# A narrow gate tile in plain fp32, in four column parts, behind the first tile of a hybrid encoder's first projection

## What is computed

```python
h = rms_norm(x, p['norm_mix'][layer])
proj = h @ p['ev_w_in'][e]
u, q, k, v, og, glr = jnp.split(proj, EV_SPLITS, axis=-1)   # 512, 256, 256, 512, 512, 32 columns
y_s5 = s5_mixer(u, ...)
y_gla = gla_mixer(q, k, v, og, glr, ...)
...
# in gla_mixer
lr = glr.astype(f32).reshape(bsz, L, 2, GLA_RANK)
logit = jnp.einsum('blzr,zrk->blzk', lr, w_gate.astype(f32)) + b_gate.astype(f32)
```

## Time and profile before

| | us |
|---|---|
| median of 3 runs (2389.73 to 2390.05) | 2390.03 |
| profiled execution | 2389.74 |
| its span, first to last instruction | 2388.0 |
| TensorE busy | 2377.4 |
| VectorE busy | 1544.8 |
| ScalarE busy | 1165.8 |
| start of the trunk's first tile on TensorE | 232.06 |

### The profile page before, as it was taken

The page is one execution under the profiler, slowest core; times in us unless marked ns, Lnnn a source line. Parts: engine busy times, 40 slices in busy tenths (PEclk is TensorE's granted clock), DMA queues, the critical chain, the costliest instruction groups (busy, mean ns, idle before and its releaser), DMA issues.

```text
span 2388.0 us, 34322 instructions
## 1 busy us (share of the span) xinstructions
PE 2377.4 (100%) x13607; PEld 2009.3 (84%) x13607; DVE 1544.8 (65%) x2616; ACT 1165.8 (49%) x2060; POOL 0.2 (0%) x4
## 2 busy tenths in 40 slices
PE   9999999999999999999999999999999999999999
PEld 6988877888889888987788888888888898888887
DVE  8999668776477876664666438958885565433332
ACT  5334455555445565545454436646764453533432
POOL 0000000000000000000000000000000000000000
PEclk9999999999999999999999999999999999999999
DMA  5435632553224654443225223232324323323322
GB/s 202 107 97 160 217 110 85 178 207 118 63 87 150 194 188 138 133 133 106 80 92 170 92 88 124 89 106 97 98 98 150 115 88 116 124 98 97 97 97 88
DMA packets 109695, 291.28 MB, mean 122 GB/s; under 512 B 18944, under 2 KB 40576, under 8 KB 108256
## 3 DMA queue, kind: packets, MB, share of 16 engines
q1 hardware_dynamic: 100832, 264.83, 34.4%
q10 hardware_dynamic: 8704, 24.25, 3.1%
HBM read 267.45 MB, written 19.50 MB: 120 GB/s over the span
## 4 chain that ended last, share of the span: by engine, by line
PE 87%; DVE 2%; ACT 1%; issue 0%; ACTq 0%
PE ps L1555 64%; PE ps L1541 5%; PE ps L1578 3%; PE ps L1546 3%; PE ps L1689 2%; PE ps L1644 2%; PE ps L1669 2%; PE ps L1716 1%; PE ps L1704 1%; PE ps L1657 0%; PE ps L1723 0%; PE ps L2093 0%; PE ps L2160 0%; PE ps L1594 0%; DVE wlo L1514 0%
## 5 line engine op out<-in xcount | busy, mean ns | idle before, releaser
L1509 ACT ACTIVATE whi<-wraw 128x1024 fp32r<-128x1024 f32 x430 | 452.1, 1052 | 202.7 <-PE ps L1555 125.3
L1514 DVE TENSOR_TENSOR wlo<-wraw,whi 128x1024 fp32r<-128x1024 f32 x430 | 522.4, 1218 | 8.1 <-ACT whi L1509 7.8
L1555 PE MATMUL ps<-in_hP,whi 128*128 128x512 f32 x1272 | 507.4, 399 | 1.7 <-DVE in_lP L1995 0.9
L1555 PE MATMUL ps<-in_hP,wlo 128*128 128x512 f32 x1272 | 495.9, 390 | 0.0
L1555 PE MATMUL ps<-in_lP,whi 128*128 128x512 f32 x1272 | 495.3, 389 | 0.0
L1555 PE MATMUL ps<-hid_P,whi 128*128 128x512 f32 x1024 | 316.8, 391 | 0.0
L1555 PEld LDWEIGHTS ps<-in_hP,whi 128*128 128x128 f32 x1272 | 238.8, 188 | 58.4 <-issue 5.9
L1555 PEld LDWEIGHTS ps<-in_hP,wlo 128*128 128x128 f32 x1272 | 238.8, 188 | 50.8
L1555 PEld LDWEIGHTS ps<-in_lP,whi 128*128 128x128 f32 x1272 | 238.9, 188 | 49.6 <-issue 1.4
L1924 DVE TENSOR_TENSOR x<-ps,x 128x256 f32<-128x256 f32 (+1 forms) x192 | 106.8, 556 | 263.0 <-PE ps L1555 261.3
L1555 PE MATMUL ps<-in_S,whi 128*128 128x256 f32 x1408 | 262.0, 287 | 0.0
(11 more groups left out here) (512 smaller groups left out, 3648.8 us busy)
## 6 DMA issues: line engine op xcount, KB each, us to landing
wraw<-wt SPq DMA_DIRECT2D x432, 512.0 KB, 3.5
wraw<-wt ACTq DMA_DIRECT2D x17, 512.0 KB, 4.2
k_scratch<-region_P SPq DMA_DIRECT2D x16, 256.0 KB, 3.1
v_scratch<-vtmp SPq DMA_DIRECT2D x32, 128.0 KB, 3.5
x<-x_in SPq DMA_DIRECT2D x4, 768.0 KB, 6.8
x<-x_in SPq DMA_DIRECT2D x2, 1536.0 KB, 7.0
mix_mem<-mem_in ACTq DMA_DIRECT2D x1, 2048.0 KB, 15.5
region_S<-k_scratch ACTq DMA_DIRECT2D x2, 1024.0 KB, 6.7
```

Of the source, the lines that this page charges most:

```text
L1509: nc.scalar.activation(whi[:, (n + 3) % NHI, :, :], wraw[:, ws(n), :, :], ACT.Copy).then_inc(wh.sem, 1)
L1514: nc.vector.tensor_tensor(wlo[:, ws(n), :, :], wraw[:, ws(n), :, :], whi[:, (n + 3) % NHI, :, :].bitcast(F32), ALU.subtract).then_inc(wr.s ...
L1555: last = nc.tensor.matmul(ps[:, bank(m), 0:N[prod.g]], w_[:, k, :], x_[:, k, :], start=(k == 0 and j == 0), stop=(k == KT - 1 and j == 2))
```

## The change

The gate's 32 columns are no longer a tile of the projection. `NT_MIX` is 16, and the gate is computed by `pe_narrow`, right behind tile 0, as plain fp32 multiplies on the fp32 input `x`. The eight k blocks are dealt to four column parts of the array: part q takes the k blocks q and q + 4 and writes partitions 32q to 32q + 31 of PSUM banks 2 and 3. So the four parts hold partial sums. They are not added in this place: `lr` has 128 partitions, is copied out in one ScalarE instruction and stored, and in the trunk L2177's successor contracts over all 128 rows with the gate weights repeated four times, which adds them. The weights `wlr` (128 KB) have a load of their own on SyncE.

Stage 0 has one tile (6), and the stages behind it have tiles 7 to 9, 10 to 12 and 13 to 15.

`act_tables` on ScalarE, between its tiles 0 and 1, makes `qf`, `qr`, `nqi` and `cneg`, with the sign as the scale of a copy; VectorE's eight copies and three negations are gone, and `dve_vv(0)` waits for ScalarE (`setup`). The memory's norm: ones become minus ones, ScalarE has one more square, and VectorE's root has two steps instead of three. `nones` moves from the trunk to the mixer. SyncE stores the gate rows before u's tiles, after a wait on `setup`. Two waits on `v_parked` are added before the first two memory multiplies, and two unused semaphores are dropped.

```diff
-NT_MIX = 17
+NT_MIX = 16
...
-            lr = sb("lr", [32, T], on=fs)
+            lr = sb("lr", [P, T], on=fs)
...
+            wlr = sb("wlr", [P, KT, 32], on=fs)
...
-                if n == NT - 1:
-                    sp.wait_ge(tf.sem, 2 * NT)
-                    sp.dma_start(lr_dram, lr[:, :]).then_inc(lr_parked.sem, 16)
...
+            def pe_narrow(pe):
+
+                pe.wait_ge(bc_l.sem, 64)
+                for z, (lo, hi) in enumerate(((0, TP), (TP, T))):
+                    for kk in range(0, KT, 4):
+                        for q in range(4):
+                            last = nc.tensor.matmul(ps[32 * q:32 * q + 32, 2 + z, 0:hi - lo], wlr[:, kk + q, :], x[:, kk + q, lo:hi],
+                                                    start=(kk == 0), stop=(kk == KT - 4))
+                last.then_inc(ssum.sem, 1)
...
+            def act_tables(a):
+
+                for i, sign in enumerate((1.0, -1.0)):
+                    nc.scalar.activation(qf[0:NS, i, :, :], pw[0:NS, i, 1:SC + 1, :], ACT.Copy, scale=sign)
+                    nc.scalar.activation(qf[NS:P, i, ::-1, :], pw[NS:P, i, 1:SC + 1, :], ACT.Copy, scale=sign)
+                    nc.scalar.activation(qr[NS:P, i, :, :], pw[NS:P, i, 0:SC, :], ACT.Copy)
+                    nc.scalar.activation(qr[0:NS, i, ::-1, :], pw[0:NS, i, 0:SC, :], ACT.Copy)
+                nc.scalar.activation(nqi[NS:P, :, :], pw[NS:P, 1, 0:SC, :], ACT.Copy, scale=-1.0)
+                nc.scalar.activation(nqi[0:NS, ::-1, :], pw[0:NS, 1, 0:SC, :], ACT.Copy, scale=-1.0)
+                a.wait_ge(bc_l.sem, 64)
+                nc.scalar.activation(cneg[:, :, :], cc[:, 1], ACT.Copy, scale=-1.0).then_inc(setup.sem, 1)
...
-                dve_chain(nc.vector.scalar_tensor_tensor(bank, bank, float(D * EPS), to, ALU.add, ALU.mult))
-                dve_chain(nc.vector.scalar_tensor_tensor(bank, bank, -0.5 / D, to, ALU.mult, ALU.mult))
+                dve_chain(nc.vector.scalar_tensor_tensor(bank, bank, -float(D * EPS), rot_w[0][:, 0:TP], ALU.add, ALU.mult))
...
-            TILES = [(6, 7), (8, 9, 10), (11, 12, 13), (14, 15, 16)]
+            TILES = [(6,), (7, 8, 9), (10, 11, 12), (13, 14, 15)]
...
+                    sp.dma_start(wlr[:, :, :], wt_in[WT["ev"] + NT][:, 0:32 * KT].rearrange("p (k n) -> p k n", k=KT)).then_inc(bc_l.sem, 16)
...
+                    sp.wait_ge(setup.sem, 1)
+                    sp.dma_start(lr_dram, lr[:, :]).then_inc(lr_parked.sem, 16)
...
-                    for n in range(4):
+                    pe_tile(pe, 0)
+                    pe_narrow(pe)
+                    for n in range(1, 4):
                         pe_tile(pe, n)
...
-                    for n in range(4):
+                    act_tile(a, 0)
+                    a.wait_ge(ssum.sem, 2)
+                    nc.scalar.activation(lr[:, :], banks(2), ACT.Copy).then_inc(setup.sem, 1)
+                    act_tables(a)
+                    for n in range(1, 4):
                         act_tile(a, n)
...
+                    v.wait_ge(setup.sem, 2)
                     dve_vv(v, 0)
...
-                    low(v, 7)
                     dve_scan(v, 0)
...
-            lr = dist[0:32, 0:T]
-            wg = acc["P"][0:32, :].rearrange("p (z n) -> p z n", z=2)
+            lr = dist[:, 0:T]
+            wg = acc["P"][:, :].rearrange("p (z n) -> p z n", z=2)
```

More of the change, by code:

```diff
@@ L139, in build @@
         gains = sb("gains", [P, 16])
+        nones = sb("nones", [P, P])[:, :]
         ps = ctx.enter_context(nc.psum_tensor("ps", [P, 8, 512], F32))
@@ L235, in mixer_in @@
             p_in, p_out = sig("m_pin"), sig("m_pout")
-            zeros = sig("m_zeros")
+            zeros, setup = sig("m_zeros"), sig("m_setup")
             sqd, acd, ssum, sroot, an, ah, ar = (sig(f"m_{n}") for n in ("sqd", "acd", "ssum", "sroot", "an", "ah", "ar"))
@@ L368, in pe_tile @@
                         for j, (w_, x_) in enumerate(((whi[:, n % NHI], in_h), (whi[:, n % NHI], in_l), (wlo[:, n % NRAW], in_h))):
-                            last = nc.tensor.matmul(ps[0:m, z, 0:hi - lo], w_[:, k, 0:m], x_[:, k, lo:hi],
+                            last = nc.tensor.matmul(ps[:, z, 0:hi - lo], w_[:, k, :], x_[:, k, lo:hi],
                                                     start=(k == 0 and j == 0), stop=(k == KT - 1 and j == 2))
@@ L712, in _ @@
                         pe.wait_ge(msq.sem, k + 1)
-                        last = nc.tensor.matmul(ps[:, 4, :], ones, early[k], start=(k == 0), stop=(k == KT - 1))
+                        last = nc.tensor.matmul(ps[:, 4, :], nones, early[k], start=(k == 0), stop=(k == KT - 1))
                     last.then_inc(msum.sem, 1)
-                    for n in range(4):
+                    pe_tile(pe, 0)
+                    pe_narrow(pe)
+                    for n in range(1, 4):
                         pe_tile(pe, n)
@@ L729, in _ @@
                     tile(6)
-                    tile(7)
                     pe_y(pe, 0)
@@ L828, in _ @@
                     nc.vector.memset(mix_h[:, 0:2, :].bitcast(F32), 0.0).then_inc(zeros.sem, 1)
+                    nc.vector.memset(nones, -1.0)
                     v.wait_ge(par_l.sem, 16)
@@ L884, in _ @@
                     low(v, 2)
[L885 to L892, removed]
+                    v.wait_ge(bc_l.sem, 64)
                     t3 = [sq3[:, 1 + i // 2, (i % 2) * 384:(i % 2) * 384 + 256].rearrange("p (g c) -> p g c", c=GC) for i in range(4)]
@@ L1051, in trunk_tail @@
             gs = {g: {n: sig(f"{n}_{g}") for n in ("sqd", "sql", "acd", "ssum", "sroot", "snew", "an", "ah", "ar", "ap", "hx",
-                                                   "qad", "tqd", "vtr", "vcp", "vca", "kvl", "kad", "ksc")} for g in "PS"}
+                                                   "qad", "tqd", "vtr", "vcp", "vca", "kvl", "kad", "ksc")
+                      if g == "P" or n not in ("kad", "ksc")} for g in "PS"}
             gs["F"] = {n: sig(f"{n}_F") for n in ("sqd", "ssum", "sroot", "snew", "an")}
@@ L2665, in tiles @@
         return a.reshape(KT, P, n, P).transpose(2, 1, 0, 3).reshape(n, P, KT * P)
-    late = {"eo": w["ev_w_out"][0], "ev": _np.concatenate([u_, q_, k_, v_, og_, glr_, _np.zeros((D, P - 32), _np.float32)], 1), "din": w["od_w_in"][0], "dout": w["od_w_out"][0]}
+    late = {"eo": w["ev_w_out"][0], "ev": _np.concatenate([u_, q_, k_, v_, og_], 1), "din": w["od_w_in"][0], "dout": w["od_w_out"][0]}
     for layer in range(DEPTH):
@@ L2674 @@
     by_token = w["od_w_in"][0][:, 2 * D:].reshape(4, 2, P, 2, 512).transpose(3, 0, 2, 1, 4).reshape(KT, P, KT * P)
-    wt = _np.concatenate([tiles(late[n]) if n != "din" else _np.concatenate([tiles(late[n])[:2 * KT], by_token], 0) for n in WT_ORDER], 0)
-    wgate = _np.zeros((2 * 16, 2, 256), _np.float32)
+    narrow = _np.zeros((1, P, KT * P), _np.float32)
+    narrow[0, :, :32 * KT] = glr_.reshape(KT, P, 32).transpose(1, 0, 2).reshape(P, 32 * KT)
+    parts = {n: tiles(late[n]) for n in WT_ORDER}
+    parts["ev"] = _np.concatenate([parts["ev"], narrow], 0)
+    wt = _np.concatenate([parts[n] if n != "din" else _np.concatenate([parts[n][:2 * KT], by_token], 0) for n in WT_ORDER], 0)
+    wgate = _np.zeros((4, 2 * 16, 2, 256), _np.float32)
     for z in range(2):
-        wgate[16 * z:16 * z + 16, z] = w["gla_w_gate"][0][z]
+        wgate[:, 16 * z:16 * z + 16, z] = w["gla_w_gate"][0][z]
+    wgate = wgate.reshape(P, 2, 256)
     j, i = _np.arange(P)[:, None], _np.arange(P)[None, :]
```

21 lines of the change are left out of this document (8 added, 13 removed).

## The result

| | before | changed |
|---|---|---|
| median of 20 runs, us | 2390.00 | 2394.28 |
| lowest and highest, us | 2389.72, 2391.26 | 2392.72, 2395.80 |
| profiled execution, us | 2389.74 | 2394.28 |
| its span, us | 2388.0 | 2392.5 |

The ratio is 1.0018, with a 95% interval from 1.0012 to 1.0024: 4.3 us slower. That is a little under the 4.8 us that was called tellable, but the whole interval lies above 1. The prediction was 2392.9 us, in a range from 2390.2 to 2396.3.

What follows compares the result with a forecast made beforehand. TensorE's queue was taken as the bound, with VectorE nearly as late at pe_y(0). Narrow tile +2.8, low -1.1, L587 -0.1, slack -0.2 and clock +1.5 gave +2.9 us: 2392.9 us, range 2390.2 to 2396.3.

Steps and rivals of the forecast that it cites:

- What bounds the place: At pe_y(0), TensorE waits 7.0 us for VectorE's states and starts at 103.9, 1.4 us later than before.
- The tile taken out: Stage 0 loses one full tile, 8.3 us of TensorE work, which turns into a wait of 7.0 us.
- the `low` that left VectorE's chain: Stage 0 on VectorE: low(7) disappears behind L587, shortening the chain to the states by 1.1 us.
- the 0.2 us of slack: At pe_y(0), TensorE started 0.23 us after VectorE's last awaited instruction; this takes 0.2 us off the sum.
- The narrow tile: Behind tile 0 on TensorE: four column parts run side by side, +2.8 us, paid nearly in full.
- Rivals 2 and 3: Narrow tile's column parts overlap only in pairs, 2395.4 us, chance 0.07; or run one after another, 2400.4 us, chance 0.05.
- rival 3: The narrow tile's four column parts run one after another, costing 10.3 us: 2400.4 us in all, chance 0.05.
- VectorE's setup: Ahead of dve_rt(0), 3.8 us leave VectorE but are worth nothing, since it then waits 6.5 us.
- Rival 4: VectorE is not the limit at pe_y(0) and TensorE keeps its saving: -5.5 us, 2384.5 us, chance 0.04.
- The trunk: In its first 6 us gate rows and weights grow fourfold; before, weights land 2.0 us after issue, so no cost expected.
- the cover of 3 us: At the trunk's start, over 3 us between the gate weights' landing before the change and their reader at 237.7.

Runs made afterwards that it cites:

- Experiment 7: The changed kernel with the dropped tile taken from the last stage instead of stage 0: 2392.95 us (1.0013).
- experiment 2: The changed kernel with all narrow multiplies in one column part instead of four: 2402.11 us (1.005 of the kernel before).
- experiment 3: The kernel before with only the tables qf, qr, nqi and cneg moved from VectorE to ScalarE, 17 tiles kept: 2389.82 us, ratio 1.0000.
- Experiment 6: The changed kernel with pe_lag(0), pe_bu(0), act_dec(0) and dve_rt(0) reordered, but tables made by VectorE as in the kernel before: 2389.51 us (0.9997).
- experiment 4: The changed kernel with pe_lag(0) between tile 4's halves, pe_bu(0) ahead of tile 5, act_dec(0) behind ScalarE's tile 4, dve_rt(0) inside dve_rot(0): 2385.47 us.
- experiment 1: The changed kernel with 29 extra multiplies, results unused, behind tile 6 to fill TensorE's wait ahead of pe_y(0): 2390.57 us (1.0002).

## Why the prediction held, step by step

**What bounds the place** was read rightly: `pe_y(0)` was to wait 7.0 us for VectorE's last memset and to start at 103.9; it waits 6.86 us and starts at 104.22. Of the 0.3 us between, 0.2 are the narrow tile's and 0.1 is tile 0's own later start (25.84 instead of 25.72), which the prediction had at nothing. The reading that mattered was the 0.23 us between two engines in the earlier trace rows, not the 65% of the earlier trace rows.

**The tile taken out** is worth 8.3 us of TensorE's work, of which 6.9 us came back as a wait, as said. The other 1.4 us are the `low` that left VectorE's chain and the 0.2 us of slack. Experiment 7 shows the same wait in another stage.

**The narrow tile** was put at 2.8 us; it costs 3.0. That it is paid nearly in full, because `pe_lag(0)` and with it VectorE's chain move along, is what experiment 2 shows: +7.7 us of work, +7.8 us of time. The Trainium skill (TensorE: Matmul & The Clock Gate, "Measured speedup vs the span model") had given an estimated 3.2 us. The measured 3.0 us lie between that and the 2.8 us of the sum; 2.7 of them pass between the first narrow record and tile 1. Rivals 2 and 3 (pairs, 5.3 us; one after another, 10.3 us) are out by the same row, and experiment 2 shows what rival 3 would look like: 10.4 us.

**VectorE's setup** was said to be worth nothing, with a wait of 6.5 us at `dve_rt(0)`; the wait is 6.9 us, and experiment 3 shows the tables' part of it apart, at 0.2 us of gain, with a ratio whose interval spans 1. No run shows the root's saved step apart. Experiment 6 adds the limit of this: it holds only as long as `pe_lag(0)` and `pe_bu(0)` stand where they do. ScalarE's copies took 5.0 us (39.10 to 44.13) instead of 4.4, and tile 1's copy started at 45.08; TensorE shows no wait there.

**Rival 4** (VectorE is not the limit) falls with the wait itself. What it named as its condition, a chain that no longer waits for `pe_lag(0)` behind tile 4, is what experiment 4 brings about, together with `pe_bu(0)` and `dve_rt(0)` moved; it then gives 2385.5 us, 1 us above the 2384.5 us of that rival.

**The trunk:** the gate weights landed 5.3 us after their issue at 237.0, not 2.0 as in the earlier trace rows, and their reader started at 242.4. Of the cover of 3 us 0.1 was left, and the weight load of that reader is listed with 0.5 us of waiting:

```profile
  PEld ps L2195: 0.5, 1
```

TensorE's matmuls show no wait there, so it cost nothing that the profile shows, but the price of four times the bytes (256 KB instead of 64) had been taken too lightly.

**What stays open:** the changed kernel's runs spread over 3.1 us (2392.72 to 2395.80), those of the kernel before over 1.5. In experiment 1, where the clock does not fall, ten of eleven lie within 0.6 us, which would fit a clock whose fall and rise differ from run to run; but experiment 4 has a spread of 2.5 us (2383.77 to 2386.23) with a granted clock of 1.00 in its profile, and there no run tells the cause. The trunk's own 2 us between traces may be part of both spreads; that is not shown.

## What to carry to other kernels

When the bounding engine is busy 100% of a stretch, look for the second latest one at each meeting point: its slack there, not its average, says what a saving is worth, and here 0.23 us of slack turned 8.3 us of saved work into a wait of 6.9. Follow the late engine's chain back through all the places where it waits itself before moving work off it. A saving ahead of such a place is worth nothing until the place moves: with `pe_lag(0)`, `pe_bu(0)` and `dve_rt(0)` all moved, the same change went from 4.3 us slower to 4.5 us faster, and with the first alone it stayed where it was. A new wait of several us on TensorE also costs clock behind it, so price it at more than its length.

## What the runs showed of the hardware

- A wait of 6.9 us put the granted clock from 1.00 to 0.50, and the first 5.8 us of work behind it ran at that level: 2.8 us lost. A wait of 6.2 us in another stage did the same (0.50 from 220 to 226, 0.51 to 228). A wait of 3.2 us lowered it too (mean 0.55 from 80 to 82, 0.59 to 84, 1.00 behind), and 1.3 us were lost.
- 29 multiplies of 512 rows whose results nobody uses kept the clock at 1.00 through the same gap (98 to 106), and 2.7 us came back.
- The granted clock can read 1.00 where multiplies plainly run slowly: 1.00 from 2.5 to 4.0 us, with 0.37 us for a multiply that takes 0.23 us later.
- Plain fp32 multiplies in four column parts overlapped over long streams, both passes included: 16 multiplies with 128 rows of contraction, 32 columns and 512 or 256 moving rows took 2.7 us, and 10.4 us in one part.
